# A transformer trunk on one core: the head of the delta rule moved into the projection and into attention

## The chip, the core and the metric

The kernel runs on one core of a Trainium2 chip. The metric is the device time of one execution in microseconds (us), the median of several runs. PE is the matmul engine (PEld its weight loads), DVE and ACT are the vector and the scalar engine, SP issues most of the DMAs. The granted clock of PE is given as a share of 2.4 GHz: 1.00 is 2.4 GHz, 0.50 is 1.2 GHz.

## The reference, cut to what matters

Two layers over 512 latent and 256 context tokens (768 in all, six tiles of 128). Each layer projects the tokens to the columns of three mixers, runs them, projects back, and then runs a mixture of 16 experts. The second layer gives no context output.

```python
def _token_mixing(h_lat, h_ctx, w_in, ...):
    cl = _split_cols(h_lat @ w_in)
    cc = _split_cols(h_ctx @ w_in)
    a_lat, a_ctx = _attention_group(cl, cc, ...)
    d_lat, d_ctx = _deltanet_group(cl, cc, ...)
    g_lat, g_ctx = _hgrn2_group(cl, cc, ...)
...
    # in _deltanet_group, before its scan over chunks:
        qkv = _short_conv(cols['dn_qkv'], conv_w)      # ends in silu
        q, k, v = jnp.split(qkv.astype(f32), 3, axis=-1)
        q = _l2norm(_heads(q, DN_HEADS)) * DN_HEAD_DIM ** -0.5
        k = _l2norm(_heads(k, DN_HEADS))
        beta = jax.nn.sigmoid(cols['dn_beta'].astype(f32))
        a = cols['dn_a'].astype(f32).reshape(b, t, 2, DN_HEADS)
        g = -jnp.exp(a_log.astype(f32)) * jax.nn.softplus(a + dt_bias.astype(f32))
```

## The kernel before, in words

Each engine has one program, written out by hand, and runs it in the order in which it is written; semaphores join them. Per layer the order is modulation, norm, input projection, attention, delta rule, HGRN, output projection, experts. On-chip tiles are views at hand-given places in one large buffer (`arena`), so stages that follow each other share room; `ps` is PSUM with eight banks.

**Projection** (`pe_proj`, `act_proj`). Twelve groups of columns, each in up to six units (a tile of tokens, or a piece of channels). A unit is 24 matmuls into bank `u % 6`, which ACT copies out. Banks 6 and 7 are free. Behind the first five units of group 10 (`G_HV`), PE turns one block each of attention's queries and keys there (`turn_qk`, L844), and ACT copies it to `qkT` (L774, L775). Group 11 is the last.

**Attention** (`pe_attention`, `dve_attention`, `act_attention`). It goes by pairs n of heads for one tile of queries: 24 pairs in layer 0 (the first 16 against six tiles of keys, the last 8, context queries, against two) and 16 in layer 1. For a pair PE turns the exponentials (`turn`, L1193), makes the next pair's scores (L1180) and then the values (L1202). DVE copies its part of the turned tiles (`evacuate`, L1122), takes the row maxima of the next pair (`row_max`, L1112) and scales the result (`finish`, L1128 and L1132). ACT copies its part of the turned tiles (L1162) and makes the next pair's exponentials (L1150). All eight banks are used: pair 0 has banks 0 to 3, pair 1 banks 4 to 7.

**The head of the delta rule** (`pe_deltanet`, `dve_deltanet`, `act_deltanet`) starts when attention's last result stands. PE turns the convolved rows `convout` to tokens (six tiles of up to six 128x128 blocks, L1525), ACT copies each tile to `dt` (L1427, L1428). DVE and ACT make the gates `bt` and `gg` (L1234 to L1242; ACT's exponential and logarithm at L1417 to L1422). DVE squares and sums queries and keys per tile (L1250, L1251), ACT makes the inverse roots `rs` (L1430, L1431, a logarithm and an exponential), DVE scales (L1261). In layer 0 PE then makes piece 0 of layer 1's modulation (16 matmuls, L1495, with weights that SP loads once `dtt` says that the rows are turned, because `dn_w` shares room with `convout`). Then PE turns queries and keys to `kqT` (L1535), ACT copies them (L1435), and DVE builds the first operand of the decays (L1269), with which the scan's own work begins (L1550, L1551).

Of the kernel before, what the change touches and what calls it, by code (L numbers as in the profile page):

```python
# [159 lines left out]
def trunk_program(nc, t):  # L160

    ctx = ExitStack()
    with ctx:
# [78 lines left out]
        w_raw = [view(6144 + 2176 * i, KT, 272) for i in range(WRING)]  # L242
        w_low = [share(f"w_low{i}", 6144 + 2176 * i, KT, 272) for i in range(WRING)]
# [15 lines left out]
        hid_row = [view(at, 512) for at in (18432, 42640)]  # L259
        mod_rows = view(42000, P)[0:96, :]  # L260
# [11 lines left out]
        dt = view(0, NT, 768)  # L272
        sq_dn = view(7680, NT, 512)
        kqT = view(4608, 2, NCH, 2, HD)
        Uc = view(7680, NCH, 2, HD)
        vnew = view(7680, NT, DNH, HD)
        S = view(9216, NCH, 2, HD)
        AT = view(10752, NT, DNH, HD)
        TR = view(12288, NT, 2, DNH, HD)
        vke = view(15360, NT, DNH, 2 * HD)  # L280
# [292 lines left out]
        def sync_program(sp):  # L573
            for layer in range(DEPTH):
# [272 lines left out]

        def pe_proj(pe, layer):
# [36 lines left out]
            for u in range(n_first, len(units)):  # L885
# [10 lines left out]
                if u >= turn_at and u < turn_at + 5:  # L896
                    turn_qk(pe, layer, u - turn_at)

# [117 lines left out]
        def dve_attention(dve, layer):  # L1016
# [117 lines left out]

            row_max(0)
            for n in range(attn_pairs(layer)):
# [3 lines left out]
                finish(n)  # L1140

        def act_attention(act, layer):
# [12 lines left out]
            for n in range(attn_pairs(layer)):  # L1155
# [8 lines left out]
                if n + 1 < attn_pairs(layer):  # L1164
                    exps(n + 1)

        def pe_attention(pe, layer):
# [39 lines left out]
            scores(0)  # L1207
            scores(1)
# [20 lines left out]
        def dve_deltanet(dve, layer):  # L1229
            dve.wait_ge(attn_y.sem, attn_y.n(layer, attn_units(layer)))  # L1230
            i0 = out_from(layer)

            alog, dtb = small[:, layer, 256:264], small[:, layer, 264:272]
            link(nc.vector.tensor_tensor(ga[:, :, :], dz[:, :, 264:272], dtb.unsqueeze(1).broadcast_to([P, NT, 8]),  # L1234
                                         ALU.add))
            link(nc.vector.tensor_scalar(gb[:, :, :], ga[:, :, :], -1.0, None, ALU.mult))
            nc.vector.tensor_tensor(gb[:, :, :], gb[:, :, :], ga[:, :, :], ALU.min).then_inc(gate_v.sem, 1)
            dve.wait_ge(gate_a.sem, gate_a.n(layer, 4))
            link(nc.vector.tensor_scalar(bt[:, :, :], bt[:, :, :], 1.0, None, ALU.add))
            nc.vector.reciprocal(bt[:, :, :], bt[:, :, :])  # L1240
            link(nc.vector.scalar_tensor_tensor(gg[:, :, :], ga[:, :, :], 0.0, gb[:, :, :], ALU.max, ALU.add))
            link(nc.vector.scalar_tensor_tensor(gg[:, :, :], gg[:, :, :], -1.0,  # L1242
                                                ealog[:, :].unsqueeze(1).broadcast_to([P, NT, 8]), ALU.mult, ALU.mult))

            for i in range(NT):
                dve.wait_ge(dtev.sem, dtev.n(layer, i + 1))
                c0, h0 = (256, 4) if i < i0 else (0, 0)
                if h0:
                    nc.vector.memset(ss[:, 8 * i:8 * i + h0], 0.0)
                link(nc.vector.tensor_tensor(sq_dn[:, i, c0:], dt[:, i, c0:512], dt[:, i, c0:512], ALU.mult))  # L1250
                ins = nc.vector.tensor_reduce(ss[:, 8 * i + h0:8 * i + 8],  # L1251
                                              sq_dn[:, i, c0:].rearrange("p (h d) -> p h d", d=HD), AX, ALU.add)
            link(ins)
            nc.vector.tensor_scalar(ss2[:, 0:48], ss[:, 0:48], EPS, None, ALU.add).then_inc(dn_ss.sem, 1)
            dve.wait_ge(dn_rs.sem, dn_rs.n(layer, 1))
            rq = rs[:, 0:48].rearrange("p (i h) -> p i h", h=8)[:, :, 0:DNH]
            link(nc.vector.tensor_scalar(rq, rq, HD ** -0.5, None, ALU.mult))
            for i in range(NT):
                c0, h0 = (256, 4) if i < i0 else (0, 0)
                v = dt[:, i, c0:512].rearrange("p (h d) -> p h d", d=HD)  # L1260
                nc.vector.tensor_tensor(v, v, rs[:, 8 * i + h0:8 * i + 8].unsqueeze(2).broadcast_to([P, 8 - h0, HD]),  # L1261
                                        ALU.mult).then_inc(dn_norm.sem, 1)
# [152 lines left out]
        def act_deltanet(act, layer):  # L1415
            i0 = out_from(layer)
            nc.scalar.activation(bt[:, :, :], dz[:, :, 256:264], ACT.Exp, scale=-1.0).then_inc(gate_a.sem, 1)  # L1417
            nc.scalar.activation(ealog[:, :], small[:, layer, 256:264], ACT.Exp).then_inc(gate_a.sem, 1)
            act.wait_ge(gate_v.sem, gate_v.n(layer, 1))
# [1151 lines left out]
```

## Time and profile before

| | |
|---|---|
| median of 3 runs | 3553.85 us (3547.67 to 3556.19) |
| the profiled execution | 3541.28 us, its span 3539.5 us |
| PE busy | 3000.9 us, 85% of the span |
| DVE busy | 2305.4 us, 65% |
| ACT busy | 1791.9 us, 51% |
| chain that ended last | PE 58%, DVE 14%, ACT 11%, issue 8%, DMA 7% |

The chain that ended last is followed back from the last instruction, at each step to what released it. The two layers are not alike in their stages, so the shares say little about one stage: the rows below are taken stage by stage.

### The profile page before, as it was taken

The numbers are of one execution on the slowest core, as the hardware profiler recorded it, in microseconds if no ns is written. First come the engines' busy times: TensorE is split into PE (matmuls) and PEld (weight loads), VectorE is DVE, ScalarE is ACT, GpSimd is POOL, SyncE is SP. The second block draws the span as 40 slices with busy tenths as digits, with TensorE's granted clock in tenths as the row PEclk, the third lists the DMA queues.
The fourth block names the chain that finished last, engine by engine and source line by source line (L and its number), as shares of the span: only waits on it lengthen the run. The fifth ranks groups of instructions, "written<-read, shape, count | busy, mean of one in ns | idle before, by whom it ended". The sixth has DMA issues, their size and how long they took to land.

```text
span 3539.5 us, 61277 instructions
## 1 busy us (share of the span) xinstructions
PE 3000.9 (85%) x25061; PEld 2297.6 (65%) x25061; DVE 2305.4 (65%) x2959; ACT 1791.9 (51%) x2346; POOL 339.8 (10%) x100
## 2 busy tenths in 40 slices
PE   7999988877886999999995999777567688888887
PEld 1698867744434666676664898677453577666676
DVE  1263665577436788878885544655763788888887
ACT  1223531223124877777774334312332588888886
POOL 0000000000001221222110000000000123223221
PEclk9999988878897999999997999778569899999998
DMA  8212010122146899999994110000013699999996
GB/s 306 82 61 72 1 49 26 32 92 96 48 159 234 321 355 358 367 351 353 366 368 173 61 60 37 1 3 3 2 49 145 250 379 370 380 376 372 378 380 243
DMA packets 212697, 686.61 MB, mean 194 GB/s; under 512 B 16011, under 2 KB 74611, under 8 KB 212369
## 3 DMA queue, kind: packets, MB, share of 16 engines
q1 hardware_dynamic: 198020, 644.16, 48.1%
q0 software_dynamic: 6144, 20.98, 2.6%
q10 hardware_dynamic: 8335, 18.56, 1.4%
q8 instruction: 158, 2.59, 0.3%
q14 instruction: 40, 0.33, 0.0%
HBM read 662.62 MB, written 21.02 MB: 193 GB/s over the span
## 4 chain that ended last, share of the span: by engine, by line
PE 58%; DVE 14%; ACT 11%; issue 8%; DMA 7%; ACTq 1%; SPq 0%; POOL 0%; DVEq 0%
PE ps L870 11%; PE ps L2202 10%; PE ps L2172 8%; PE ps L1573 6%; PE ps L1969 4%; ACT hi L2280 4%; DMA gu<-in_moe_w_up 3%; PE ps L1202 3%; DVE gu_lo L2430 2%; ACT arena L2289 2%; DMA gu<-in_moe_w_gate 2%; PE ps L2210 2%; PE ps L809 2%; PE ps L1874 2%; PE ps L1895 1%
## 5 line engine op out<-in xcount | busy, mean ns | idle before, releaser
L2430 DVE TENSOR_TENSOR gu_lo<-gu,hi 128x2816 fp32r<-128x2816 f32 x256 | 783.1, 3090 | 227.7 <-ACT hi L2280 183.5
L2280 ACT ACTIVATE hi<-gu 128x2816 fp32r<-128x2816 f32 x256 | 644.0, 2551 | 165.5 <-DMA gu<-in_moe_w_up 128.2
L2172 PE MATMUL ps<-hi,xsplit 128*96 128x512 f32 (+3 forms) x2304 | 563.6, 390 | 44.2 <-DVE arena L2444 15.8
L2172 PEld LDWEIGHTS ps<-hi,xsplit 128*96 128x96 f32 (+1 forms) x2304 | 397.0, 177 | 159.3 <-ACT hi L2280 23.1
L2430 DVE TENSOR_TENSOR down_lo<-down,hi 128x1024 fp32r<-128x1024 f32 (+1 forms) x256 | 401.5, 1618 | 63.5 <-ACT hi L2280 63.4
L2172 PE MATMUL ps<-gu_lo,xsplit 128*96 128x512 f32 (+3 forms) x1536 | 387.6, 389 | 40.1 <-DVE gu_lo L2430 40.1
L2280 ACT ACTIVATE hi<-down 128x1024 fp32r<-128x1024 f32 (+1 forms) x256 | 343.3, 1379 | 124.4 <-PE ps L2202 124.4
L2172 PEld LDWEIGHTS ps<-gu_lo,xsplit 128*96 128x96 f32 (+1 forms) x1536 | 268.3, 181 | 132.7 <-DVE gu_lo L2430 72.2
L1573 PE MATMUL ps<-arena 64*64 64x64 f32 (+1 forms) x6080 | 206.2, 225 | 33.7 <-DVE arena L1306 21.4
L2510 POOL DMA_INDIRECT arena<-xn_rows,row_of x32 | 41.4, 1293 | 1924.6 <-DVE row_of L2423 1920.0
L1573 PEld LDWEIGHTS ps<-arena 64*64 64x64 f32 x6080 | 196.5, 137 | 42.3 <-DVE arena L1306 24.2
L2532 POOL DMA_INDIRECT out<-arena,row_of x16 | 138.7, 8668 | 551.4 <-DVE arena L2444 551.4
L767 ACT ACTIVATE arena<-ps 128x256 f32<-128x256 f32 (+3 forms) x132 | 48.4, 384 | 276.5 <-PE ps L870 276.5
L2532 POOL DMA_INDIRECT x_rows<-arena,row_of x16 | 105.6, 6598 | 574.4 <-DVE arena L2450 574.4
L563 DVE TENSOR_TENSOR w_low<-arena,w_high 128x2048 fp32r<-128x2048 f32 (+1 forms) x24 | 55.2, 2302 | 159.7 <-ACT w_high L556 159.6
L1461 ACT ACTIVATE arena<-ps 128x256 f32<-128x256 f32 x120 | 46.0, 384 | 194.9 <-PE ps L1573 193.3
L1895 PE MATMUL ps<-arena 64*64 64x64 f32 x2240 | 84.3, 263 | 69.2 <-DVE arena L1735 69.2
L1969 PE MATMUL ps<-arena 128*128 128x512 f32 x320 | 140.6, 602 | 0.0
L2289 ACT ACTIVATE arena<-ps,modC 128x64 f32<-128x64 f32 (+1 forms) x384 | 113.2, 420 | 41.9 <-PE ps L2140 41.5
L1895 PEld LDWEIGHTS ps<-arena 64*64 64x64 f32 x2240 | 76.4, 171 | 85.7 <-issue 63.2
L2210 PE MATMUL ps<-const,arena 128*128 128x64 f32 x704 | 101.8, 311 | 35.6 <-ACT arena L2308 34.5
L2202 PE MATMUL ps<-hi,hTm 128*96 128x512 f32 x352 | 112.0, 399 | 19.4 <-DVE hTm_lo L2482 14.9
(319 smaller groups left out, 5069.9 us busy)
## 6 DMA issues: line engine op xcount, KB each, us to landing
gu<-in_moe_w_gate SPq DMA_DIRECT2D x256, 704.0 KB, 15.5
gu<-in_moe_w_up SPq DMA_DIRECT2D x256, 704.0 KB, 5.2
down<-in_moe_w_down SPq DMA_DIRECT2D x64, 2048.0 KB, 13.6
down<-in_moe_w_down SPq DMA_DIRECT2D x32, 1536.0 KB, 17.0
arena<-in_w_mod SPq DMA_DIRECT2D x12, 2048.0 KB, 11.6
arena<-in_w_in SPq DMA_DIRECT2D x22, 1024.0 KB, 5.2
arena<-in_w_mod SPq DMA_DIRECT2D x15, 1024.0 KB, 5.2
arena<-in_w_mod SPq DMA_DIRECT2D x18, 512.0 KB, 3.8
```

The source lines that it names most:

```text
L870: ins = nc.tensor.matmul(ps[:, u % 6, n0:n], lhsT=lhs, rhs=rhs, start=(part == 0 and f == 0), stop=(part == 2 and f == KT - 1))
L1202: ins = nc.tensor.matmul(ps[:, unit_bank(n, kv), 0:HD], lhsT=probT[kv][:, kt * P:(kt + 1) * P], rhs=vtok[:, kt, kv * HD:(kv + 1) * HD], st ...
L1573: ins = nc.tensor.matmul(ps[HB[par], bank, c0 + width * h:c0 + width * (h + 1)], lhsT=lhs[HB[par], i, h, :], rhs=rhs(par, h), start=True, ...
L1895: ins = nc.tensor.matmul(ps[HB[c % 2], 2 * (n % 3) + hb, c // 2 * HD:c // 2 * HD + HD], lhsT=a, rhs=b, start=True, stop=True)
L1969: ins = nc.tensor.matmul(ps[:, u % 6, :], lhsT=yT[:, f, i * P:(i + 1) * P], rhs=w[:, f, :], start=(f == 0), stop=(f == KT - 1))
L2172: ins = nc.tensor.matmul(ps[0:lhs.shape[1], 3 * m + b, 0:n], lhsT=lhs, rhs=w[:, c0 + 512 * b:c0 + 512 * b + n], start=(row == 0 and stage ...
L2202: ins = nc.tensor.matmul(ps[0:lhs.shape[1], y_bank + half, :], lhsT=lhs, rhs=w[:, c0:c0 + 512], start=(ft == 0 and stage == 0 and n == 0), ...
L2210: nc.tensor.matmul(ps[:, 6 + ft // 8, (ft % 8) * CAP_L:(ft % 8 + 1) * CAP_L], lhsT=source[:, ft * P:(ft + 1) * P], rhs=cst("ident64"), sta ...
L2280: nc.scalar.activation(hi_part(p, is_last), whole(p), ACT.Copy).then_inc(hi_a.sem, 1)
L2289: ins = nc.scalar.activation(xe[:, f, c0:c0 + n], ps[:, bank, at:at + n], ACT.Identity, scale=modC[:, 3, f, v:v + 1], bias=modC[:, 2, f, v ...
L2430: nc.vector.tensor_tensor(lo_part(p), whole(p), hi_part(p, is_last).bitcast(F32), ALU.subtract) \
L2532: nc.gpsimd.indirect_dma_start(out=table, out_offset=bass.IndirectOffsetOnAxis(ap=row_of[0:rows_e, e:e + 1].bitcast(U32), axis=0), in_=ye[ ...
```

## The change

The work of the delta rule's head is not changed, its place is. The six tiles of rows are turned by PE behind the last unit of group 10 and the units of group 11, through banks 6 and 7 (`dt_tiles`, `turn_conv`); in layer 1, where group 11 has only four units, the last two tiles both stand behind the last unit. Attention's second pair of heads waits for their copies, since it uses those banks. Gates, squares, roots and scaling are cut in pieces, which stand behind given pairs of attention on DVE and ACT. Piece 0 of the modulation stays ahead of the turning of queries and keys. Tiles are laid elsewhere in the arena so that `dt` is free of attention's tiles; the modulation's rows get a place of their own (`dn_row`), on which HGRN waits; and the first load of projection weights waits for one more modulation group.

```diff
-        w_raw = [view(6144 + 2176 * i, KT, 272) for i in range(WRING)]
+        w_raw = [view(at, KT, 272) for at in (8320, 6144)]
...
-        dt = view(0, NT, 768)
+        dt = view(9728, NT, 768)
...
-                        sp.wait_ge(modmm.sem, modmm.n(layer, N_MOD - MRING + g + 1))
+                        sp.wait_ge(modmm.sem, modmm.n(layer, N_MOD - MRING + 2))
...
+                for i in dt_tiles(layer, u):
+                    act.wait_ge(dtt.sem, dtt.n(layer, i + 1))
+                    c1 = 256 if i < out_from(layer) else 0
+                    nc.scalar.activation(dt[:, i, c1:512], ps[:, 6, c1:512], ACT.Copy)
+                    nc.scalar.activation(dt[:, i, 512:768], ps[:, 7, 0:256], ACT.Copy).then_inc(dtev.sem, 1)
...
+        def dt_tiles(layer, u):
+
+            first, last = unit_at(layer, G_HV + 1) - 1, unit_at(layer, len(GROUPS)) - 1
+            if u < first:
+                return []
+            return [u - first] * (u - first < NT) if u < last else list(range(u - first, NT))
+
+        def turn_conv(pe, layer, i):
+
+            if i == 0:
+                pe.wait_ge(qktev.sem, qktev.n(layer, 5))
+                pe.wait_ge(convact.sem, convact.n(layer, 6))
+            else:
+                pe.wait_ge(dtev.sem, dtev.n(layer, i))
+            c0 = i * P if i < NT_CTX else i * P + 4
+            for j in range(2 if i < out_from(layer) else 0, 6):
+                ins = nc.tensor.transpose(ps[:, 6 + j // 4, (j % 4) * P:(j % 4 + 1) * P], convout[:, j, c0:c0 + P], ident)
+            ins.then_inc(dtt.sem, 1)
...
+                for i in dt_tiles(layer, u):
+                    turn_conv(pe, layer, i)
...
                 finish(n)
+                if n == 0:
+                    gates_begin()
+                if n == 3:
+                    gates_end()
+                if 1 <= n < 1 + NT:
+                    key_squares(n - 1)
+                if 10 <= n < 10 + NT:
+                    key_norm(n - 10)
...
+                if n == 0:
+                    nc.scalar.activation(bt[:, :, :], dz[:, :, 256:264], ACT.Exp, scale=-1.0).then_inc(gate_a.sem, 1)
+                    nc.scalar.activation(ealog[:, :], small[:, layer, 256:264], ACT.Exp).then_inc(gate_a.sem, 1)
+                if n == 1:
+                    act.wait_ge(gate_v.sem, gate_v.n(layer, 1))
+                    nc.scalar.activation(gb[:, :, :], gb[:, :, :], ACT.Exp).then_inc(gate_a.sem, 1)
+                    act.wait_ge(gate_a.sem, gate_a.n(layer, 3))
+                    nc.scalar.activation(gb[:, :, :], gb[:, :, :], ACT.Ln, bias=1.0).then_inc(gate_a.sem, 1)
+                if n == 8:
+                    act.wait_ge(dn_ss.sem, dn_ss.n(layer, 1))
+                    link_act(nc.scalar.activation(rs[:, 0:48], ss2[:, 0:48], ACT.Ln))
+                    nc.scalar.activation(rs[:, 0:48], rs[:, 0:48], ACT.Exp, scale=-0.5).then_inc(dn_rs.sem, 1)
...
             scores(0)
+            pe.wait_ge(dtev.sem, dtev.n(layer, 6))
             scores(1)
```

`gates_begin` and `gates_end` are the three and four small operations of L1234 to L1242, `key_squares(i)` is L1249 to L1254 for one tile, `key_norm(i)` is L1257 (once) and L1261 for one tile.

Three places show how instructions move. The first is PE at the end of layer 1's projection. L870 before and L896 after are the projection's matmuls, L1180 and L1267 attention's scores, L871 is `turn_conv`. Before:

```order
L870 MATMUL ps<-w_high_57,h_high 128x256 x8
L870 MATMUL ps<-w_high_57,h_low 128x256 x8
L870 MATMUL ps<-w_low_54,h_high 128x256 x8
L1180 MATMUL ps<-arena 128x512 x2
```

Now:

```order
L871 MATMUL ps<-const,arena 128x128 x6
L896 MATMUL ps<-w_high_57,h_high 128x256 x8
L896 MATMUL ps<-w_high_57,h_low 128x256 x8
L896 MATMUL ps<-w_low_54,h_high 128x256 x8
L871 MATMUL ps<-const,arena 128x128 x12
L1267 MATMUL ps<-arena 128x512 x2
```

A tile's six blocks now stand between two units, and twelve, two tiles, between the last unit and the first scores. The second place is PE at the end of layer 0's attention. L1202 and L1289 are the last values, L1495 and L1537 piece 0 of the modulation, L1535 and L1567 the turning of queries and keys. Before:

```order
L1193 MATMUL ps<-const,arena 128x128 x4
L1202 MATMUL ps<-arena 128x64 x4
L1525 MATMUL ps<-const,arena 128x128 x36
L1495 MATMUL ps<-arena,condT 2x128 x16
L1535 MATMUL ps<-const,arena 128x128 x24
```

Now:

```order
L1280 MATMUL ps<-const,arena 128x128 x4
L1289 MATMUL ps<-arena 128x64 x4
L1537 MATMUL ps<-arena,condT 2x128 x16
L1567 MATMUL ps<-const,arena 128x128 x24
```

The 36 blocks of rows are gone from there. The third place is ACT around pair 8 of layer 0. L1150 before and L1224 after are the exponentials, L1162 and L1236 the copies of turned tiles, L1251 and L1252 the root of the key norms. Before:

```order
L1162 ACTIVATE arena<-ps 128x512 x2
L1150 ACTIVATE arena,rsum<-ps,nmax 128x768 x2
L1162 ACTIVATE arena<-ps 128x512 x2
L1150 ACTIVATE arena,rsum<-ps,nmax 128x768 x2
```

Now:

```order
L1224 ACTIVATE arena,rsum<-ps,nmax 128x768 x2
L1251 ACT_TABLE_LOAD
L1251 ACTIVATE rs<-ss 128x48
L1252 ACT_TABLE_LOAD
L1252 ACTIVATE rs<-rs 128x48
L1236 ACTIVATE arena<-ps 128x512 x2
```

Two table loads and two small operations stand between the exponentials and the copies that follow. Behind pair 1 there is another such place, with one table load for the logarithm and one ahead of the next exponentials.

## Rows read from the trace of the kernel before

**Rows 1.** Windows: length, busy PE, PEld, DVE, ACT, POOL (records), granted clock, DMA share, GB/s
```profile
342.50:455.20 112.70, 110.36 (x832) 87.99 (x832) 67.92 (x169) 63.48 (x148) 0.00 (x0) 1.00 0.08 29
466.00:468.00 2.00, 2.00 (x12) 1.21 (x10) 0.91 (x3) 0.97 (x2) 0.00 (x0) 0.50 0.12 37
478.00:480.00 2.00, 2.00 (x9) 1.91 (x9) 0.00 (x0) 0.30 (x1) 0.00 (x0) 0.50 0.00 0
498.00:500.00 2.00, 2.00 (x31) 1.49 (x26) 1.93 (x9) 0.00 (x0) 0.00 (x0) 1.00 0.39 115
```

**Rows 2.** Timeline, one pair of attention, layer 0: start, us, engine, line, [idle before <-releaser]
```profile
376.41 2.89 PE L1202 MATMUL ps<-arena 128*128 128x64 f32 x24
...
378.41 0.89 ACT L1150 ACTIVATE arena<-ps,nmax 128x768 f32<-128x768 f32 x1
...
379.14 1.48 PE L1193 MATMUL ps<-const,arena 128*128 128x128 f32 x12
...
379.34 0.28 DVE L1132 TENSOR_SCALAR arena<-ps,rinv 128x64 f32<-128x64 f32 x1 [0.60 <-PE ps L1202]
380.00 0.42 DVE L1122 COPY arena<-ps 128x256 f32<-128x256 f32 x1 [0.38 <-PE ps L1193]
380.00 1.25 ACT L1162 ACTIVATE arena<-ps 128x512 f32<-128x512 f32 x2 [0.60 <-PE ps L1193]
...
382.04 1.22 PE L1202 MATMUL ps<-arena 128*128 128x64 f32 x9
382.15 0.96 DVE L1112 TENSOR_REDUCE nmax<-ps 128x1 f32<-128x768 f32 x1 [1.08 <-PE ps L1180]
```

**Rows 3.** Timeline of layer 0's head, on PE and DVE
```profile
454.49 0.67 DVE L1132 TENSOR_SCALAR arena<-ps,rinv 128x64 f32<-128x64 f32 x2 [0.35 <-PE ps L1202]
...
465.23 6.43 PE L1495 MATMUL ps<-arena,condT 128*2 128x128 f32 x32 [4.31 <-DMA arena<-in_w_mod]
...
471.59 3.23 PE L1535 MATMUL ps<-const,arena 128*128 128x128 f32 x24
...
475.74 2.10 DVE L1269 TENSOR_TENSOR arena<-const,gg 128x256 f32<-128x256 f32 x6 [2.99 <-ACT arena L1435]
...
490.59 1.66 PE L1495 MATMUL ps<-arena,condT 128*2 128x128 f32 x7
```

**Rows 4.** Timeline of layer 1's head
```profile
2232.58 0.28 DVE L1132 TENSOR_SCALAR arena<-ps,rinv 128x64 f32<-128x64 f32 x1 [0.98 <-PE ps L1202]
...
2246.28 3.85 PE L1535 MATMUL ps<-const,arena 128*128 128x128 f32 x20 [8.09 <-DVE arena L1261]
...
2250.98 2.10 DVE L1269 TENSOR_TENSOR arena<-const,gg 128x256 f32<-128x256 f32 x6 [2.10 <-ACT arena L1435]
```

**Rows 5.** Timeline of a modulation piece at full clock, PE
```profile
498.41 1.91 PE L1495 MATMUL ps<-arena,condT 128*2 128x128 f32 x16
```

**Rows 6.** Timeline of the projection, layer 0, where a block of queries is turned
```profile
321.75 0.82 PE L844 MATMUL ps<-const,arena 128*128 128x128 f32 x6
...
322.32 1.19 PE L870 MATMUL ps<-w_high,h_high 128*128 128x256 f32 x8
...
323.09 0.38 ACT L775 ACTIVATE arena<-ps 128x256 f32<-128x256 f32 x1
```

**Rows 7.** Timeline of layer 0's head: gates, squares, root, scaling
```profile
457.73 0.19 DVE L1239 TENSOR_SCALAR bt<-bt 128x48 f32<-128x48 f32 x1 [1.87 <-ACT gb L1422]
...
458.75 0.69 DVE L1250 TENSOR_TENSOR arena<-arena 128x512 f32<-128x512 f32 x1
...
460.08 0.68 DVE L1250 TENSOR_TENSOR arena<-arena 128x512 f32<-128x512 f32 x1
...
467.27 1.28 ACT L1431 ACT_TABLE_LOAD   x1
468.57 0.24 ACT L1431 ACTIVATE rs<-rs 128x48 f32<-128x48 f32 x1
...
469.06 3.70 DVE L1261 TENSOR_TENSOR arena<-arena,rs 128x512 f32<-128x512 f32 x6
```

More of the change, by code:

```diff
@@ L259, in trunk_program @@
         hid_row = [view(at, 512) for at in (18432, 42640)]
+        dn_row = [view(at, 512) for at in (9216, 42640)]
         mod_rows = view(42000, P)[0:96, :]
@@ L271, in trunk_program @@
         convout = view(38984, 6, 772)
-        dt = view(0, NT, 768)
[L273 to L280, printed above, removed]
+        dt = view(9728, NT, 768)
+        sq_dn = [view(7168 + 512 * i, 512) for i in range(2)]
+        kqT = view(0, 2, NCH, 2, HD)
+        Uc = view(3072, NCH, 2, HD)
+        vnew = view(3072, NT, DNH, HD)
+        S = view(4608, NCH, 2, HD)
+        AT = view(17408, NT, DNH, HD)
+        TR = view(6144, NT, 2, DNH, HD)
+        vke = view(14336, NT, DNH, 2 * HD)
         NTm = view(18944, NT, DNH, HD)
@@ L1133, in finish, with gates_begin @@
                                             rinv[:, 2 * n + kv:2 * n + kv + 1], None, ALU.mult).then_inc(attn_y.sem, 1)
+            def gates_begin():
+                dtb = small[:, layer, 264:272]
+                link(nc.vector.tensor_tensor(ga[:, :, :], dz[:, :, 264:272], dtb.unsqueeze(1).broadcast_to([P, NT, 8]),
+                                             ALU.add))
+                link(nc.vector.tensor_scalar(gb[:, :, :], ga[:, :, :], -1.0, None, ALU.mult))
+                nc.vector.tensor_tensor(gb[:, :, :], gb[:, :, :], ga[:, :, :], ALU.min).then_inc(gate_v.sem, 1)
@@ new lines, in key_squares @@
+            def key_squares(i):
+                dve.wait_ge(dtev.sem, dtev.n(layer, i + 1))
+                c1, h0 = (256, 4) if i < i0 else (0, 0)
+                if h0:
+                    nc.vector.memset(ss[:, 8 * i:8 * i + h0], 0.0)
+                link(nc.vector.tensor_tensor(sq_dn[i % 2][:, c1:], dt[:, i, c1:512], dt[:, i, c1:512], ALU.mult))
+                ins = nc.vector.tensor_reduce(ss[:, 8 * i + h0:8 * i + 8],
+                                              sq_dn[i % 2][:, c1:].rearrange("p (h d) -> p h d", d=HD), AX, ALU.add)
+                if i == NT - 1:
+                    link(ins)
+                    nc.vector.tensor_scalar(ss2[:, 0:48], ss[:, 0:48], EPS, None, ALU.add).then_inc(dn_ss.sem, 1)
@@ new lines, in key_norm @@
+            def key_norm(i):
+                if i == 0:
+                    dve.wait_ge(dn_rs.sem, dn_rs.n(layer, 1))
+                    rq = rs[:, 0:48].rearrange("p (i h) -> p i h", h=8)[:, :, 0:DNH]
+                    link(nc.vector.tensor_scalar(rq, rq, HD ** -0.5, None, ALU.mult))
+                c1, h0 = (256, 4) if i < i0 else (0, 0)
+                v = dt[:, i, c1:512].rearrange("p (h d) -> p h d", d=HD)
+                nc.vector.tensor_tensor(v, v, rs[:, 8 * i + h0:8 * i + 8].unsqueeze(2).broadcast_to([P, 8 - h0, HD]),
+                                        ALU.mult).then_inc(dn_norm.sem, 1)
@@ L1231, in dve_deltanet @@
             i0 = out_from(layer)
[L1233 to L1262, printed above, removed]
             dve.wait_ge(kqtev.sem, kqtev.n(layer, 6))
@@ L1512, in act_piece @@
             act.wait_ge(modmm.sem, modmm.n(1, DN_FIRST[g + 1]))
[L1513 to L1514 removed]
+            nc.scalar.activation(dn_row[g % 2][0:2, 0:n], ps[0:2, 7, 0:n], ACT.Copy).then_inc(modadd.sem, 1)
+            act_store(act, dn_row[g % 2], g + 1, 128 * DN_FIRST[g], n)
         def pe_deltanet(pe, layer):
             pe.wait_ge(attn_y.sem, attn_y.n(layer, attn_units(layer)))
[L1518 removed]
             i0 = out_from(layer)
[L1520 to L1527 removed]
             pe_piece(pe, layer, 0, 0, 16)
[L1529 removed]
             for i in range(NT):
@@ L1692, in dve_hgrn @@
                 nc.vector.memset(gpad[:, :, :, 0:1], 0.0)
+                if layer < DEPTH - 1 and d == 0:
+                    dve.wait_ge(modout.sem, 16 * 5)
                 link(nc.vector.memset(Ah[:, :, i0:], 0.0))
@@ L1839, in act_hgrn @@
                 exps(0)
+                if layer < DEPTH - 1 and d == 0:
+                    act.wait_ge(modout.sem, 16 * 5)
                 for j in range(2):
```

44 lines of the change are left out of this document (12 added, 32 removed).

## The prediction

> **What bounds the kernel now.** I read the windows first, stage by stage. In layer 0's attention PE is busy 110.36 of 112.70 us at a granted clock of 1.00, DVE 67.92 and ACT 63.48 [rows 1]: attention is PE's, and the two others have room in it. How much room, and where, is read from the timeline of one pair [rows 2]. Then I read the head of the delta rule, in both layers [rows 3, 4]: the reader is to see that no engine is the bound there. It is a chain of small steps handed from engine to engine.
>
> In layer 0 the last result of attention ends at 454.49 + 0.67 = 455.16, and the first operand of the decays starts at 475.74: 20.6 us. PE waits 4.31 us for the modulation's weights, spends 6.43 us on piece 0, and starts the turning of queries and keys only at 471.59 [rows 3]. In layer 1, where there is no piece, it is 2232.86 to 2250.98, 18.1 us, with PE idle 8.09 us for DVE's scaled rows [rows 4]. The projection's end is PE's too: between a turned block of queries and the next product nothing is lost [rows 6].
>
> **The change part by part, as a sum.** All against the profiled execution, 3541.28 us, which lies 12.6 us under the median; I take the same difference off the median.
>
> Head, layer 0. What stays behind attention is piece 0, then the turning of queries and keys with ACT's copies. Its weights are asked for at the end of the projection, some 110 us earlier, so the 4.31 us are gone. The piece took 6.43 us at a clock of 0.50 [rows 1, 3], after an idle PE. Now PE comes straight from attention at 1.00, and half as many records took 1.91 us at that clock [rows 1, 5], so 3.8 us. Bounds: 3.2 (half of 6.43) and 6.4. From the turning to the first operand of the decays it was 475.74 - 471.59 = 4.15 us, ACT's copies for the most part. New head 3.8 + 4.15 = 8.0 us against 20.6: **12.6 us gained**, 10.0 if the piece runs at half clock.
>
> Head, layer 1. Only the turning is left. It took 2250.98 - 2246.28 = 4.70 us [rows 4], paced in part by DVE's scaling, which will long be done. I take 4.0, a little under layer 0's 4.15 since it has 20 blocks for 24; bounds 3.5 and 4.7. **14.1 us gained.**
>
> Projection, cost. A block set of six costs PE 322.32 - 321.75 = 0.57 us between two products [rows 6]; a set of four by that 0.38. ACT's two copies are done 323.47 - 321.75 = 1.72 us after the turning starts, inside the next product, so the next tile finds its banks free. Layer 0: 6 x 0.57 = 3.4 us. Layer 1: 2 x 0.38 + 2 x 0.57 = 1.9, and the last two tiles behind the last unit, where the second waits for the copies of the first: 1.72 + 0.57 = 2.3. Behind the second come attention's first scores, into other banks, and under them its copies end. The new wait before pair 1's scores so costs nothing; without that cover it would be about 1.2 us. **3.4 + 4.2 = 7.6 us lost.**
>
> Attention, DVE's pieces. A pair takes 382.04 - 376.41 = 5.63 us. DVE ends `finish` at 379.62, then has two copies of 0.42 to make and starts the next row maxima at 382.15, which is 1.69 us of free time. PE needs the first copy at 382.04 [rows 2]. One tile's squares and sums are 460.08 - 458.75 = 1.33 us [rows 7]: the first copy ends at 379.62 + 1.33 + 0.42 = 381.37, in time, and both copies before the maxima are due. So they cost nothing, as do the tiles of scaling at 3.70 / 6 = 0.62. At pair 3 the end of the gates (458.75 - 457.73 = 1.02) stands ahead of a tile's squares: 2.35 us, the copy ends at 382.39, and PE waits 0.35 us. The maxima then are 0.7 late; ACT's second exponentials ended at 379.30, and are wanted halfway through the turning that starts at 379.14, about 0.5 us later, which with PE's own 0.35 covers it.
>
> Attention, ACT's pieces. A table load with what follows is 468.57 - 467.27 = 1.30 us, a small operation 0.24 [rows 7]. ACT is free at about 379.5 and its copies start at 380.00 [rows 2]. Pair 8: two loads and two operations, 3.1 us, put the copies at 382.6, the first ends at 383.2, and PE wanted it at 382.04: 1.1 us. Pair 1: exponential, load, logarithm, 1.8 us; the first copy ends at 381.9, just in time; then the table goes back ahead of the next exponentials, which start 0.65 late against 0.5 of slack: 0.15. Queued behind ACT there are the copies and through them PE's values, nothing else. Pair 0's two exponentials (0.5) fit. Per layer 0.35 + 1.1 + 0.15 = 1.6, **3.2 us lost** in two layers.
>
> Of this price the Trainium skill says something else ("ScalarE: Activation LUTs", What ACT_TABLE_LOAD costs): a switch of tables is 1283 ns for the load and about 1380 ns for a drain, 2.66 us in all. The row here has the 1283 ns and no drain, the operation starts 0.02 us behind the load. By the page's figure the sum would be some 8 us worse, the second rival below.
>
> At no cost I take: the load of the first projection weights that waits for one more modulation group (nothing needs them for several groups' time: PE still has two groups and the turning of the normed rows to do; uncovered it is the time of one load), the moved tiles, and HGRN's new wait on the stored modulation rows, whose last piece is stored a whole output stage earlier (uncovered it is one small store).
>
> Sum: 12.6 + 14.1 - 7.6 - 3.2 = **15.9 us less**: 3525.4 for a profiled run like that of before, and 3553.85 - 15.9 = 3538.0 for the median, 0.45%. What this kernel's measurement can tell from no change is about 0.3%, 10.7 us, so 3543.2 and above is no change.
>
> **Rivals.**
> 1. *More of PE at full clock behind the head.* The stage of the decays (475.74 to 490.59, 14.9 us) ran mostly at 0.50 [rows 1, 3]; it had PE idle just before it. With less idle before, part of it could run at 1.00; at most half of it goes, 7.4 us a layer. Against it: the fall came while PE was already back at work, in a stage of matmuls of four columns and 2 us windows with PE busy throughout. Half of the most, 7 us over both layers: 3531. Chance 0.12.
> 2. *A table switch costs more than its row when copies stand behind it.* The switches of the head had little queued behind them; attention's will. No row has a load with copies due behind it, so I price it at the load once more, 1.28 us each [rows 7]: pair 1 then costs 1.4 and pair 8 3.7 in place of 0.15 and 1.1, 3.9 more a layer, 7.8 in all: 3545.8, no change. Chance 0.08.
> 3. *The pieces lie on attention's loop by half.* If the free time of 1.69 us is in truth needed (a wait that this profile puts down to another), half of DVE's added 0.7 + 1.0 + 6 x 1.33 + 0.2 + 3.7 = 13.6 us in layer 0 and about 12 in layer 1 is exposed, 12.8 us: 3550.8, no change. Against it the idle gaps are in the rows of every pair. Chance 0.09.
> 4. *They lie on it wholly, and it ends slower.* DVE's copies and row maxima would be what PE waits for in every pair that has a piece. DVE's 25.6 and ACT's 2 x 6.2 us (four loads and five to six small operations a layer) are then all paid, in place of my 3.2: 3538.0 + 25.6 + 12.4 - 3.2 = 3572.8, slower. The point from which it decides: with 12 tile pieces a layer, 24 in all, 15.9 / 24 = 0.66 us lost per piece eats the gain, and 1.1 us makes it slower by 0.3%. Chance 0.05.
> 5. *The change doesn't do what it says*: PE at the end of attention still waits (weights, a late root), or the time saved is waited for again at the next wait, in HGRN or at the experts' weights: 3554. Against it, all loads behind the head are asked for by progress, not by time. Chance 0.06.
>
> My forecast has 0.60.
>
> **How the numbers follow.** The forecast's own range is 3532 to 3545 (the piece at half clock, layer 1's turning at 4.7, ACT's copies a little later, and 4 us that the runs of before spread to either side). The range for 8 in 10 takes in rival 1 and most of rivals 2 and 3: 3530 to 3550. Faster by over 0.3%: 0.93 of the forecast and all of rival 1, 0.68. Within 0.3%: rivals 2, 3 and 5 and the forecast's tail, 0.27. Slower by over 0.3%: rival 4, 0.05.
>
> **What the changed profile would show.** From the last scaled result of attention to the decays' first operand, 8.0 us in layer 0 and 4.0 in layer 1, with no DMA wait at piece 0 and that piece in about 3.8 us. Six turnings of rows between layer 0's last products at 0.57 us each; in layer 1 a PE wait of about 1.1 us between the last two tiles. Pairs of 5.63 us, but pair 3 longer by 0.35, pair 8 by 1.1. I am wrong if pairs 1 to 6 or 10 to 15 are longer than their neighbours, if a table load in attention is followed by a gap, if the exponentials wait for their load, or if the stages behind the head, which I take as unchanged, differ by more than a few us.

## The result and the profile after

The changed kernel takes 3526.22 us (median of 7 runs, 3518.28 to 3532.9) against 3547.67 us for the kernel before (7 runs, 3540.22 to 3556.19): a ratio of 0.9937, 95% interval 0.9923 to 0.9951. It is faster by 21.5 us, where 15.9 had been forecast, and the time lies below the range's lower end of 3530.

| | before | after |
|---|---|---|
| profiled execution | 3541.28 us, span 3539.5 us | 3526.22 us, span 3524.4 us |
| PE busy | 3000.9 us | 2992.9 us, 85% |
| DVE busy | 2305.4 us | 2301.7 us, 65% |
| ACT busy | 1791.9 us | 1796.9 us, 51% |

Hardly any work is gone. The two profiled executions differ by 15.1 us; 8.0 of these are in PE's busy time, with as many matmuls (25061) in both. Busy time also goes with the granted clock under the work: piece 0 alone is 6.43 us before and 5.32 after. The rest is idle time of PE. First the head of layer 0 after, in the timeline (start, us, engine, line, idle time before and its releaser); it answers to [rows 3]:

```profile
462.04 0.67 DVE L1160 TENSOR_SCALAR arena<-ps,rinv 128x64 f32<-128x64 f32 x2 [0.36 <-PE ps L1289]
...
462.76 5.32 PE L1537 MATMUL ps<-arena,condT 128*2 128x128 f32 x32 [0.38 <-DVE arena L1160]
...
468.02 3.23 PE L1567 MATMUL ps<-const,arena 128*128 128x128 f32 x24
468.71 3.42 ACT L1477 ACTIVATE arena<-ps 128x256 f32<-128x256 f32 x12 [7.12 <-PE ps L1567]
...
472.24 2.10 DVE L1326 TENSOR_TENSOR arena<-const,gg 128x256 f32<-128x256 f32 x6 [9.53 <-ACT arena L1477]
```

PE goes from attention's last result straight into piece 0, without the 4.31 us for weights, and then into the turning. The operand starts 9.53 us behind attention, where it was 20.6. The piece took 5.32 us and not 3.8: the windows of the same stretch (length, busy PE, PEld, DVE, ACT, POOL, granted clock, DMA share, GB/s) show the clock falling to 0.50 under it. Why it fell there, in one trace of six, is not known.

```profile
460.00:462.00 2.00, 1.87 (x14) 1.29 (x13) 1.27 (x7) 1.34 (x6) 0.00 (x0) 1.00 0.00 0
462.00:464.00 2.00, 1.62 (x11) 0.99 (x11) 0.57 (x2) 0.00 (x0) 0.00 (x0) 0.70 0.03 8
464.00:466.00 2.00, 2.00 (x11) 1.24 (x10) 0.00 (x0) 0.00 (x0) 0.00 (x0) 0.50 0.00 0
```

Layer 1's head, in the timeline, answers to [rows 4]. PE no longer waits 8.09 us for DVE, and from 2231.75 + 0.28 to 2235.64 it is 3.6 us, where it was 18.1:

```profile
2231.75 0.28 DVE L1160 TENSOR_SCALAR arena<-ps,rinv 128x64 f32<-128x64 f32 x1 [0.99 <-PE ps L1289]
...
2232.09 2.56 PE L1567 MATMUL ps<-const,arena 128*128 128x128 f32 x20 [0.38 <-DVE arena L1160]
...
2235.64 2.10 DVE L1326 TENSOR_TENSOR arena<-const,gg 128x256 f32<-128x256 f32 x6 [3.01 <-ACT arena L1477]
```

The price stands in three places of the timeline. At the end of layer 1's projection the last tile waits for the copies of the one before:

```profile
2134.80 0.82 PE L871 MATMUL ps<-const,arena 128*128 128x128 f32 x6
...
2135.66 0.60 ACT L780 ACTIVATE arena<-ps 128x512 f32<-128x512 f32 x1 [0.27 <-PE ps L871]
2136.15 0.38 ACT L781 ACTIVATE arena<-ps 128x256 f32<-128x256 f32 x1
...
2136.58 0.87 PE L871 MATMUL ps<-const,arena 128*128 128x128 f32 x6 [0.96 <-ACT arena L781]
...
2137.39 2.85 PE L1267 MATMUL ps<-arena 64*128 64x512 f32 x16
```

Behind pair 8 of layer 0 ACT loads two tables, and PE's values wait for the copies queued behind them (the pair is 409.10 - 402.47 = 6.63 us long, the others 5.63):

```profile
402.74 1.28 ACT L1251 ACT_TABLE_LOAD   x1
...
404.04 0.24 ACT L1251 ACTIVATE rs<-ss 128x48 f32<-128x48 f32 x1
404.30 1.28 ACT L1252 ACT_TABLE_LOAD   x1
...
405.59 0.24 ACT L1252 ACTIVATE rs<-rs 128x48 f32<-128x48 f32 x1
405.74 1.06 ACT L1236 ACTIVATE arena<-ps 128x512 f32<-128x512 f32 x2
406.37 2.75 PEld L1289 LDWEIGHTS ps<-arena 128*128 128x128 f32 x24 [1.33 <-ACT arena L1236]
406.37 2.89 PE L1289 MATMUL ps<-arena 128*128 128x64 f32 x24 [0.93 <-ACT arena L1236]
```

And behind pair 3 the chain that ended last leaves PE for DVE, through the end of the gates, a tile's squares and the first copy, before the next pair's values can start at 377.25:

```profile
374.57 0.45 DVE bt L1174
...
375.37 0.70 DVE arena L1184
...
376.69 0.43 DVE arena L1150
```

**By stages.** Single executions of one kernel differ by 20 to 30 us, so I measured each stage in several traces of each kernel, from the starts of the same instructions: the first product of the projection, the first scores, attention's last scaled result, the decays' first operand, HGRN's first operation, the output's first turned block and the last squares of the second norm. Means in us (one trace gives every stage to 0.1):

```
stage                            before (5 traces)    changed (6 traces)     difference
start to the first projection    132.1 (131.8-132.2)  133.7 (132.4-134.9)    +1.6
projection, layer 0              211.1 (210.9-211.4)  215.0 (214.8-215.3)    +3.9
attention, layer 0               112.0 (111.9-112.0)  113.5 (113.4-113.5)    +1.5
head, layer 0                     20.8 ( 20.4- 21.0)    8.4 (  8.1-  9.8)   -12.4
scan, layer 0                    275.9 (275.9-275.9)  274.9 (273.2-276.0)    -1.0
projection, layer 1              184.9 (184.6-185.2)  189.0 (188.8-189.1)    +4.1
attention, layer 1                91.3 ( 91.3- 91.4)   93.8 ( 92.7- 94.4)    +2.5
head, layer 1                     18.6 ( 18.3- 19.0)    3.9 (  3.8-  3.9)   -14.7
scan, layer 1                    266.1 (265.3-266.9)  264.5 (263.7-265.3)    -1.6
HGRN, output, experts, both     2233.0 (2228-2240)   2229.4 (2223-2235)     -3.6
sum of the six touched           638.7 (638.5-638.8)  623.5 (621.8-625.2)   -15.2
all the rest                    2907.1 (2901-2915)   2902.5 (2893-2909)      -4.6
```

The touched stages give 15.2 us. Each repeats to a few tenths, but for the changed kernel's head in layer 0 and its attention in layer 1, where the clock fell in some of the traces. All the rest is 4.6 us shorter in the mean, with single traces spread over 15 us.

### The profile page after: what moved, and what is told of

It is laid out like the page before. It is cut to its first block, busy times and chain, and to the rows that moved or that the text cites. A ratio compares the mean times of both kernels' runs of the same rounds, so it can differ in the third digit from the quotient of the medians.

```text
span 3524.4 us, 61283 instructions
## 1 busy us (share of the span) xinstructions
PE 2992.9 (85%) x25061; PEld 2294.6 (65%) x25061; DVE 2301.7 (65%) x2959; ACT 1796.9 (51%) x2350; POOL 339.9 (10%) x100
## 4 chain that ended last, share of the span: by engine, by line
PE 58%; DVE 14%; ACT 10%; issue 8%; DMA 7%; ACTq 1%; SPq 0%; POOL 0%; DVEq 0%
PE ps L896 11%; PE ps L2238 10%; PE ps L2208 9%; PE ps L1605 6%; PE ps L2005 4%; ACT hi L2316 4%; DMA gu<-in_moe_w_gate 3%; DMA gu<-in_moe_w_up 3%; PE ps L1289 2%; DVE gu_lo L2466 2%; PE ps L815 2%; ACT arena L2325 2%; PE ps L2246 2%; PE ps L1910 1%; PE ps L1931 1%
```

## The experiments

**The two kernels again.** The first question was whether 21.5 us is the size of the change at all. I ran both kernels again without an edit, before four more times and the changed one five more, each in five rounds, on three chips.

> The kernel before, unchanged, against itself: ratio 1.000, and a second trace of it. The two profiled executions so far differ by 15.1 us (span 3539.5 to 3524.4), the medians of seven runs by 21.5 us. Theory A: the profiled run of before was a short one of its kernel, and the further 6 us are spread of executions that comes from stages that the change doesn't touch; then this second trace is longer than the first (span 3543 to 3552), with its head stages (20.6 and 18.1 us) and its pairs of 5.63 us the same to 0.3 us, and the difference lies in modulation, scan or expert stages where the granted clock or the DMAs differ. Theory B: the change saves 6 us more somewhere behind the head (a later stage that runs at another clock because it starts otherwise); then both traces of before have the same stage that is longer than in both traces of after.

Measured: 3547.27 us, ratio 0.9997 (0.9985 to 1.0009).

> The changed kernel, unchanged. Ratio to before: theory A, that my sum holds and the rest is spread, 0.9945 to 0.9965 in these rounds (12 to 20 us); theory B, that there is more behind the head, 0.992 to 0.9945. In its trace, by both: heads of 9.5 and 3.6 us again, attention of layer 0 at 113.7 us. Whether the clock falls in piece 0 of layer 0 (5.32 us in place of 3.8) and behind pair 8 of layer 1 (2.3 us in place of 1.0) is the same here if it follows from the work, and may differ if it hangs on the moment.

Measured: 3530.28 us, ratio 0.9942 (0.9927 to 0.9956). Its head in layer 0 is 8.1 us long and piece 0 takes 3.66 us, at a clock of 1.00 (timeline, then the window inside it):

```profile
461.63 3.66 PE L1537 MATMUL ps<-arena,condT 128*2 128x128 f32 x32 [0.38 <-DVE arena L1160]
...
469.44 2.10 DVE L1326 TENSOR_TENSOR arena<-const,gg 128x256 f32<-128x256 f32 x6 [7.86 <-ACT arena L1477]
```

```profile
462.00:464.00 2.00, 2.00 (x21) 1.56 (x19) 0.00 (x0) 0.00 (x0) 0.00 (x0) 1.00 0.00 0
```

> The kernel before again, for a third trace and more rounds. Open is 7 us: the stages that the change touches are 13.3 and 14.2 us shorter in the two traces of the changed kernel, the rounds say 21. Theory A: the rest of the program is the same in both kernels and varies by its own (2896 to 2912 us in ten traces); with more rounds the ratio of the changed kernel goes up to 0.995 to 0.996. Theory B: the rest is some 7 us shorter in the changed kernel; the ratio stays at 0.994 and the traces of before have a rest of 2904 to 2912, those of the changed kernel of 2896 to 2905.

Measured: 3549.22 us, ratio 1.0014 (1.0002 to 1.0025).

> As the run ahead of it: a fourth trace of before, and a second null ratio, 1.000 by both theories. Touched stages at 638.5 us to 0.3.

Measured: 3546.87 us, ratio 1.0004 (0.9995 to 1.0013).

> The changed kernel, third trace. Theory A: ratio 0.995 to 0.9965, rest of the program anywhere in 2896 to 2912. Theory B: ratio 0.9935 to 0.9945, rest under 2905. Touched stages 623 to 625.5 us, by whether the clock falls in piece 0 and behind pair 8 of layer 1.

Measured: 3531.93 us, ratio 0.996 (0.9947 to 0.9973).

> As the run ahead of it, a fourth trace of the changed kernel and rounds of its own; by theory A a ratio of 0.995 to 0.9965, by theory B of 0.9935 to 0.9945.

Measured: 3527.47 us, ratio 0.9949 (0.9932 to 0.9967).

> A fifth trace of before. If the rest of the program differs by kernel: 2905 to 2912, scan stages of 275.9 and 265.3 to 266.9 us as in the four so far. If it is spread alone, anywhere in 2893 to 2915.

Measured: 3545.09 us, ratio 0.9993 (0.9979 to 1.0007).

> A fifth trace of the changed kernel and rounds of its own. If the 5 us are the kernel's: ratio 0.994 to 0.995, rest under 2905, scans of 273 to 276 and 263.7 to 264.7. If they are spread: 0.995 to 0.9965, and a rest as before's.

Measured: 3533.94 us, ratio 0.9944 (0.9927 to 0.9962).

> As the run ahead of it, a sixth trace of the changed kernel; the ratio 0.994 to 0.995 if 5 us are the kernel's, 0.995 to 0.9965 if they are spread.

Measured: 3526.02 us, ratio 0.9932 (0.9917 to 0.9948).

All together, 128 executions of before have a mean of 3547.3 us and 36 of the changed kernel 3527.9: 19.4 us less, 95% interval 17.3 to 21.5. One interval of the unchanged kernel leaves 1 out, and the changed kernel's ratios go from 0.9932 to 0.996, so one ratio here is good to some 0.15%, 5 us, and no better. Of the 21.5 us, 2.1 are therefore the chance of seven runs; 19.4 is the size to explain. The expectations had two theories: A, that the touched stages (15.2 us) are all there is, and B, that some 6 us more are behind the head. The interval from 17.3 leaves A out: 4.2 us, 2.1 to 6.3, are gained outside the touched stages.

**Rows alone.** The rows are turned in the projection as in the change; gates, squares, roots and scaling go back to the head.

```diff
@@ dve_attention
-                if n == 0:
-                    gates_begin()
-                if n == 3:
-                    gates_end()
-                if 1 <= n < 1 + NT:
-                    key_squares(n - 1)
-                if 10 <= n < 10 + NT:
-                    key_norm(n - 10)
@@ dve_deltanet
+            gates_begin()
+            gates_end()
+            for i in range(NT):
+                key_squares(i)
+            for i in range(NT):
+                key_norm(i)
```

(ACT's six operations go back with them, to the start of `act_deltanet`.)

> Only the turning of rows is moved into the projection; gates, squares, root and scaling stay in the head, in the order of before. My theory: DVE's own chain (455.16 to 469.06 in layer 0, 2232.86 to 2245.71 in layer 1, with hardly a wait for the rows in it) sets the head, so that moving the rows alone gains some 2 us in layer 0 (PE is no longer late with the piece: 18.7 in place of 20.6 us) and nothing in layer 1 (18 us), and costs 7.6 us in the projection: slower by 5 to 6 us, ratio 1.0015. Rival: that the wait for turned rows and for the weights sets the head; then it keeps most of the 26 us and is faster by 8 or more, ratio 0.998 or less.

Measured: 3556.64 us, ratio 1.0024 (1.0013 to 1.0034), mean 8.1 us over before. The projections cost what they cost in the change (214.8 and 188.9 us), attention is as before (112.0 and 91.3), and the heads are 20.4 and 18.9 us, as long as ever. Its timeline shows why: DVE's chain sets the head's end, and PE stands for 10.94 us ahead of the turning of queries and keys.

```profile
458.54 3.66 PE L1537 MATMUL ps<-arena,condT 128*2 128x128 f32 x32 [0.38 <-DVE arena L1200]
...
472.39 3.70 DVE L1080 TENSOR_TENSOR arena<-arena,rs 128x512 f32<-128x512 f32 x6
...
473.13 4.60 PE L1567 MATMUL ps<-const,arena 128*128 128x128 f32 x24 [10.94 <-DVE arena L1080]
```

The wait for weights is gone here and piece 0 is short, and nothing comes of it. The 2 us that the expectation still gave layer 0 did not come: the turning of queries and keys is now paced by the scaling, 4.60 us where it was 3.23 [rows 3]. Rows alone are a loss. Gates and roots without the rows were not run; the squares need the turned rows.

**Twice the squares behind a pair.** This asks how much room a pair has on DVE: 2 x 1.33 = 2.66 us against the 1.69 read from [rows 2].

```diff
-                if n == 3:
+                if n == 7:
                     gates_end()
-                if 1 <= n < 1 + NT:
-                    key_squares(n - 1)
+                if 1 <= n < 4:
+                    key_squares(2 * n - 2)
+                    key_squares(2 * n - 1)
```

> The changed kernel with two tiles of squares behind each of pairs 1 to 3 (in place of one behind pairs 1 to 6), the end of the gates behind pair 7. My theory of the room in a pair: DVE has 1.69 us free, and PE waits from the point at which the first copy is late. Two tiles are 2.66 us, the first copy ends 0.66 late, so pairs 1 to 3 are 0.6 to 0.7 us longer each, pair 7 as others, and attention of layer 0 some 1.6 us longer than with the changed kernel. Rival (DVE's work is on the loop): each of these pairs longer by 1.3 more than in the changed kernel, pairs 4 to 6 shorter by as much, the sum unchanged. Rival (DVE is never in the way): pairs of 5.63 us.

Measured in one execution (3542.15 us): layer 0's attention is 115.4 us against 113.5, 1.9 more. PE waits for DVE's copy behind each of the three pairs; this is the first:

```profile
364.49 0.75 DVE L1150 COPY arena<-ps 128x256 f32<-128x256 f32 x2
365.05 2.86 PE L1290 MATMUL ps<-arena 128*128 128x64 f32 x24 [0.63 <-DVE arena L1150]
```

From one pair's values to the next it is 6.33, 6.30 and 6.52 us in place of 5.63, 5.63 and 6.02 (the last had the end of the gates, which is now at pair 7 and costs nothing there). One tile per pair cost nothing, two cost 0.70, 0.67 and 0.89 us over 5.63, where the expectation had 0.6 to 0.7 each. The room that this shows is the one up to the first copy, 382.04 - 0.42 - 379.62 = 2.00 us by [rows 2], from which 2.66 stand out by 0.66; the 1.69 us up to the row maxima is not what PE waits for. Layer 1's attention is 97.5 us where it was 92.7 to 94.4, and 1.6 us of this are a fall of the clock behind the late pairs.

**Piece 0 behind the turning.**

```diff
-            pe_piece(pe, layer, 0, 0, 16)
             for i in range(NT):
                 pe.wait_ge(dn_norm.sem, dn_norm.n(layer, i + 1))
...
+            pe_piece(pe, layer, 0, 0, 16)
             pe.wait_ge(kqtev.sem, kqtev.n(layer, 6))
```

> The changed kernel with piece 0 of layer 0 behind the turning of queries and keys, where PE idles 1.5 us for DVE's first operand. The head of layer 0 then is about 3.9 us to the first operand of the decays (as layer 1's 3.6), and the piece's 3.8 us at full clock (5.3 if the clock falls in it) come after: with 1.5 of it in the gap the products of the decays start 2.3 to 3.8 us behind the operand in place of 0.57. Net for layer 0 from attention's end to those products: 6.6 to 7.8 us in place of 8.5 to 10.1. Rival: the piece runs at half clock there and nothing is won.

Measured in one execution (3523.96 us); the timeline of its head:

```profile
460.50 3.23 PE L1566 MATMUL ps<-const,arena 128*128 128x128 f32 x24 [0.38 <-DVE arena L1160]
...
463.65 3.66 PE L1537 MATMUL ps<-arena,condT 128*2 128x128 f32 x32
...
467.24 1.06 PE L1582 MATMUL ps<-gg,const 128*128 128x4 f32 x8
```

The operand's start is 4.5 us behind attention in place of 8.1, but that marker flatters this edit, since the piece now lies behind it. The first product of the decays is the fairer one: 467.24 - 460.44 = 6.8 us behind attention's end, where the changed kernel needs 8.4 (it comes 0.57 behind the operand there). So at that point the edit is worth 1.6 us: ACT's copies and DVE's operand now run under the piece. In this trace the lead then grows. DVE's first operation of HGRN comes 277.1 us behind attention's end, and 280.3 in the second changed run: 3.2 us. In between, the windows have a granted clock of 0.50 from 472 to 484 us here and from 472 to 488 there. Whether the second half of the gain belongs to the edit, one trace does not show.

**The root over two pairs.** One table load and one operation stand behind pair 8. The second load then comes ahead of the next exponentials, and the second operation behind them, at pair 9.

```diff
                     link_act(nc.scalar.activation(rs[:, 0:48], ss2[:, 0:48], ACT.Ln))
+                if n == 9:
                     nc.scalar.activation(rs[:, 0:48], rs[:, 0:48], ACT.Exp, scale=-0.5).then_inc(dn_rs.sem, 1)
```

> The changed kernel with the root's logarithm behind pair 8 and its exponential behind pair 9, so that the table goes back ahead of attention's own exponentials, as it does behind pair 1. My reading of pair 8 (ACT's copies come 1.0 us late because two loads and two operations, 3.1 us, stand ahead of them): the pair of 6.6 us in layer 0 goes back to 5.6 to 5.8, and in layer 1, where behind the late pair PE's clock fell for some 3.4 us and the two pairs together took 2.4 us more, all of it goes with the cause. Attention of layer 0 1.0 us shorter, of layer 1 2.2 to 2.4 us. Rival (the clock falls by itself there): layer 1 wins 1.0 only.

Measured in one execution (3518.28 us): attention 112.5 us in layer 0 (113.5) and 91.7 in layer 1 (94.4 in four traces of the changed kernel, 92.7 in two). The 1.0 us is pair 8's stall. The other 1.7 of layer 1 is a fall of PE's clock that came behind that stall in the changed kernel, here in the windows of the trace profiled with the result:

```profile
2194.00:2196.00 2.00, 1.23 (x11) 1.24 (x12) 1.78 (x3) 2.00 (x6) 0.00 (x0) 1.00 0.00 0
2196.00:2198.00 2.00, 2.00 (x15) 2.00 (x15) 0.28 (x1) 0.96 (x3) 0.00 (x0) 0.70 0.00 0
2198.00:2200.00 2.00, 2.00 (x11) 2.00 (x11) 0.63 (x2) 0.34 (x1) 0.00 (x0) 0.50 0.00 0
2200.00:2202.00 2.00, 2.00 (x13) 1.07 (x11) 0.51 (x2) 0.85 (x2) 0.00 (x0) 0.95 0.00 0
```

PE waited 0.93 us up to 2194.77, and some 2 us later it worked at 1.2 GHz for about 3.4 us. Layer 0 has the same stall and stays at 1.00. One trace without the fall would show little, since two of the changed kernel's six have none either. Over all traces of this document, nine have the stall behind layer 1's pair 8 and five of them the fall behind it; nine have no such stall (before, rows alone, this run and the joined kernel) and none has the fall.

**The last two tiles of layer 1.** The first of them is turned two thirds into the last unit, so that its copies lie under the last products.

```diff
                     ins = product(u, part)
+                    if part == 1 and u == len(units) - 1 and len(dt_tiles(layer, u)) == 2:
+                        turn_conv(pe, layer, 4)
...
-                for i in dt_tiles(layer, u):
+                for i in dt_tiles(layer, u)[-1:]:
                     turn_conv(pe, layer, i)
```

> The changed kernel with layer 1's tile 4 turned two thirds into the last unit, tile 5 behind it. The PE wait of 0.96 us between the two tiles is gone but for 0.2: from the first product of layer 1's projection to attention's first scores 0.7 to 0.8 us less. Rival: ACT's queue (the copies now stand ahead of a unit's copy) makes the last unit late, no gain.

(ACT copies this tile ahead of the last unit's own copy.) Measured in one execution (3533.31 us): layer 1's projection 188.3 us against 189.0. The wait of 0.96 us is gone, 0.6 to 0.7 of it as time.

**All three joined**, with the end of the gates moved from pair 3 to pair 7.

> All three, and the end of the gates behind pair 7 in place of pair 3 (which took 0.36 us in each layer). By my prices 2.5 + 3.4 + 0.75 + 0.7 = 7 us less than the changed kernel in the stages touched; in the timed rounds 4 to 10 us less, ratio to before 0.990 to 0.993. Theory A of the spread (the stages that the change doesn't touch vary by 15 us from one execution to the next, whatever the kernel) expects these stages, as in all traces so far, at 2896 to 2912 us, with no order by kernel.

Measured: 3521.52 us, ratio 0.9925 (0.9908 to 0.9942).

> The joined kernel again. Touched stages 615.4 us as in its first trace, 8 us under the changed kernel's mean of 623.3; if the rest is alike, its median is 7 to 8 us under that of the changed kernel in these same rounds, ratio to before 0.991 to 0.993. If the rest follows what stands ahead of it, it differs from that by more than 3 us.

Measured: 3525.48 us, ratio 0.9919 (0.9903 to 0.9935). The eleven executions have a mean of 3522.0: 25.4 us (22.7 to 28.1) under before and 5.9 us (2.7 to 9.1) under the changed kernel. The touched stages say 615.0 against 623.5, which is 8.5 us. If 2.0 of these are only the marker of the piece (3.6 shown for 1.6) it is 6.5. Both lie within the interval. In the joined kernel's timeline no wait is left between the projection and attention:

```profile
2133.43 0.82 PE L876 MATMUL ps<-const,arena 128*128 128x128 f32 x6
2134.00 1.19 PE L901 MATMUL ps<-w_low,h_high 128*128 128x256 f32 x8
2135.21 0.88 PE L876 MATMUL ps<-const,arena 128*128 128x128 f32 x6
2136.01 2.85 PE L1275 MATMUL ps<-arena 64*128 64x512 f32 x16
```

## Why the prediction was wrong in the time and right in the mechanism

**The sum.** Forecast for the touched stages 15.9 us, found 15.2. Term by term: head of layer 0 12.6 against 12.4; head of layer 1 14.1 against 14.7; projection 3.4 and 4.2 against 3.9 and 4.1; attention 1.6 and 1.6 against 1.5 and 2.5. A set of six blocks costs about 0.65 us in layer 0 (3.9 / 6), not 0.57: the 0.57 reach only to the start of the next product, whose first eight matmuls then take 1.19 us [rows 6] where others take 1.11. Pair 3 was longer by 0.36 (0.35 forecast), pair 8 by 1.0 (1.1), and pair 1 by nothing (0.15). In layer 1's head the turning took 2.56 us where it had been 3.85. Two things are gone there, the pacing by the scaling, which the sum had seen, and a clock of 0.50, which it had not: before, the windows have 0.50 from 2244 to 2249 us under the turning, and the changed kernel has 1.00. How much is due to each isn't shown. What the forecast had not seen in attention is the fall of the clock behind layer 1's pair 8, 1.7 us in four traces of six, which comes only where the stall is.

**The step that failed** is the one ahead of the sum: "I take the same difference off the median". The median of three runs shown, 3553.85 us, lies 6.5 us above the mean of 128 executions, and with four more runs of before the median was 3547.67. Of the 11.8 us by which 3538.0 was too high, 6.2 are this base, 2.1 the chance of the changed kernel's seven runs, and the other 3.5 are gain that the sum did not have. With 3547.3 as the base my sum gives 3531.4, inside the range and 3.5 us above the changed kernel's mean of 3527.9. The prediction knew of two bases, the profiled 3541.28 and the median, 12.6 us apart, and allowed 4 us for their spread, which was too little.

**The second step** is smaller: "the stages behind the head, which I take as unchanged". Of the 19.4 us, 4.2 are not in the touched stages. 2.6 are in the two scans. In layer 0 the place can be read. About 165 us into the scan PE has nothing to do for two microseconds, and behind that its clock falls; windows of before:

```profile
638.00:640.00 2.00, 0.00 (x0) 0.00 (x0) 1.93 (x8) 0.00 (x0) 0.00 (x0) 1.00 0.67 200
640.00:642.00 2.00, 1.15 (x32) 1.04 (x32) 2.00 (x8) 0.00 (x0) 0.00 (x0) 0.90 0.21 64
642.00:644.00 2.00, 1.16 (x22) 1.19 (x24) 1.70 (x7) 0.00 (x0) 0.00 (x0) 0.50 0.00 0
...
648.00:650.00 2.00, 2.00 (x42) 2.00 (x40) 1.01 (x4) 0.77 (x2) 0.00 (x0) 0.50 0.00 0
```

and of the changed kernel in a run whose scan took 273.2 us (the fourth one):

```profile
632.00:634.00 2.00, 0.18 (x8) 0.00 (x0) 1.93 (x8) 0.25 (x1) 0.00 (x0) 1.00 0.56 161
...
636.00:638.00 2.00, 1.11 (x21) 1.14 (x23) 1.75 (x6) 0.00 (x0) 0.00 (x0) 0.56 0.03 8
638.00:640.00 2.00, 2.00 (x48) 2.00 (x45) 1.73 (x5) 0.00 (x0) 0.00 (x0) 0.59 0.00 0
640.00:642.00 2.00, 0.97 (x32) 0.83 (x30) 2.00 (x7) 0.02 (x1) 0.00 (x0) 1.00 0.00 0
```

Before, the clock is still at 0.50 in the window ten microseconds behind the idle one; in the second it is back at 1.00 after eight. Up to ACT's copy of a modulation row 162 us into the scan the two run alike, and at the next one they are 2.7 us apart (259.5 and 256.8 us), which is the whole of 275.9 against 273.2. All five traces of before took 275.9 us, and three of the changed kernel's six less. That the change moves the scan's start, and with it where the fall lies, is only argued. It isn't shown. The stage ahead of the projection is 1.6 us longer, in the trace profiled with the result in part by a clock of 0.50 in the window 122 to 124 us, where before and the second changed run have 1.00. No load stands in the chain from 94.9 us to the first product in either kernel, so the later load of weights was not waited for, as taken. The rest, some 3 us less in HGRN, output and experts, is smaller than what one kernel shows of itself, and stays open.

**The rivals.** *More of PE at full clock behind the head* fell as I had priced it: in layer 0 the clock fell 2 us behind the operand in before and in the second changed run, and the first 162 us of the scan are equal to 0.1 us in these two. In layer 1 it fell 2.1 to 3.4 us behind the operand where it had been 1.7 in the profiled run of before, worth at most 1.7 of the 7 us. From the operand to DVE's next step behind it the time is 16.3 us in the mean of before and 15.0 in the changed kernel, most of what layer 1's scan gained, but it is 14.3 in the run of rows alone, whose head is as long as before's. So a shorter head is not needed for it. *A table switch costs more than its row* fell: both loads took 1.28 us, and the first operation started 0.02 us behind its load (404.04 to 402.74 + 1.28), the copies right behind the second. The Trainium skill ("ScalarE: Activation LUTs", What ACT_TABLE_LOAD costs) gives 1283 ns for the load, which the trace confirms, and about 1380 ns more for a drain, which none of the loads shown here has. *The pieces lie on attention's loop*, by half or wholly, fell with attention's +1.5 us and with the run of two tiles a pair, which would have cost nothing more had they been wholly paid already. *The change doesn't do what it says* fell with both heads.

**Clock of piece 0.** Five of six traces have the 3.66 us that I took (3.8), the one profiled with the result 5.32, inside the bounds of 3.2 and 6.4.

## What to carry to other kernels

Build the forecast on a base that as many executions as possible give: here the median of three runs was off by 6.5 us, and no term of the sum was off by more than 1. A chain of small steps can be priced step by step to about half a microsecond from the timeline, falls of the clock aside, if the room on each engine is read off one period of the loop that is to hide it. What has to move is the step that sets the chain's end: with the rows alone, which were not that step, the kernel was slower (1.0024), and with gates and norms moved too it was faster. What is left then are stalls of about a microsecond where two hidden pieces meet, and taking three of these out, with piece 0 put under ACT's copies, gave 5.9 us more.

## What was unexpected

Behind a stall of 0.93 us of PE in a loop at full clock came a stretch of about 3.4 us at 1.2 GHz some 2 us later, in layer 1 in four traces of six, in layer 0 with the same stall in none, and nowhere without the stall. Where it comes, a stall of 1.0 us costs 2.7. What decides whether it comes is open.

One kernel's executions spread over 30 us (before: 3531.28 to 3561.28), and not evenly over the stages: in before, layer 0's scan was 275.9 us in all five traces and the touched stages agree within 0.3 us, while layer 0's output stage takes 103.7, 108.0 or 109.7 us (to 0.1) and its experts 928.8 to 938.0. A stage table over a few traces so resolves a change of 1 us that 36 executions resolve only to 2.
